# A feed-forward down projection as seven block products, with weight sums on GpSimd

## What is computed

```python
def swiglu(x, w_gate, w_up, w_down):
    return (jax.nn.silu(x @ w_gate) * (x @ w_up)) @ w_down
...
for l in range(DEPTH):
    x = layer_norm(ALPHA * x + FFN_RESIDUAL * swiglu(x, ffn1_w_gate[l], ffn1_w_up[l], ffn1_w_down[l]), ...)
    h = x @ w_in[l]
    ...
    oa = stick_breaking_attention(...)
    ob = chunked_rel_attention(..., rel_bias[l])
    mixed = jnp.concatenate([head_rmsnorm(oa, sb_out_g[l]), head_rmsnorm(ob, ca_out_g[l])], axis=-1)
    x = layer_norm(ALPHA * x + mixed @ w_out[l], ln2_g[l], ln2_b[l])
    x = layer_norm(ALPHA * x + FFN_RESIDUAL * swiglu(x, ffn2_w_gate[l], ffn2_w_up[l], ffn2_w_down[l]), ...)
```

## Time and profile before

| | |
|---|---|
| median of 3 runs | 1040.13 us |
| lowest, highest | 1039.67, 1041.14 us |
| span of the profiled execution (first to last instruction) | 1038.6 us |
| TensorE (PE) busy | 1020.4 us, 98% |
| VectorE (DVE) busy | 585.2 us, 56% |
| ScalarE (ACT) busy | 503.7 us, 49% |
| GpSimd (POOL) busy | 28.3 us, 3% |
| mean granted TensorE clock | 0.998 |

### The profile page before, as it was taken

One profiled execution on the slowest core, in us unless ns is written; L12 is line 12 of the kernel. 1 busy time (PEld: TensorE's weight loads), 2 busy tenths in 40 slices (PEclk: granted clock), 3 DMA queues, 4 the chain that ended last, 5 costly groups with the idle time before them and its releaser, 6 DMA issues.

```text
span 1038.6 us, 18030 instructions
## 1 busy us (share of the span) xinstructions
PE 1020.4 (98%) x7128; PEld 943.2 (91%) x7128; DVE 585.2 (56%) x562; ACT 503.7 (49%) x552; POOL 28.3 (3%) x56
## 2 busy tenths in 40 slices
PE   6999999999999999999989999999999999999999
PEld 6999999799987999999889999997999889999997
DVE  4544544755788554544655454457457975444447
ACT  5444343557685344343543434346576754434335
POOL 3000000001100000000000000000010000000000
PEclk9999999999999999999999999999999999999999
DMA  8755555363325555555455545553623265545451
GB/s 333 282 195 185 179 201 166 119 244 122 123 82 209 202 197 174 189 190 175 161 198 210 185 180 201 172 192 129 232 88 122 87 239 203 187 179 198 171 195 42
DMA packets 34338, 185.24 MB, mean 178 GB/s; under 512 B 3824, under 2 KB 3824, under 8 KB 19440
## 3 DMA queue, kind: packets, MB, share of 16 engines
q1 hardware_dynamic: 32400, 174.60, 47.6%
q0 software_dynamic: 1744, 9.45, 2.5%
q10 hardware_dynamic: 144, 0.52, 0.1%
HBM read 183.51 MB, written 1.05 MB: 178 GB/s over the span
## 4 chain that ended last, share of the span: by engine, by line
PE 98%; DMA 1%; issue 1%; ACT 1%; DVE 0%; SPq 0%; ACTq 0%; DVEq 0%
PE bank L893 29%; PE bank L894 29%; PE bank L895 29%; PE bank L991 8%; PE bank L955 1%; PE bank L938 1%; DMA raw<-stream 1%; PE bank L1107 1%; ACT scratch L407 0%; PE bank L949 0%; DVE xn L715 0%; DVE xT_lo L660 0%; ACT xT_hi L398 0%; ACT w_hi L624 0%; ACT lt L410 0%
## 5 line engine op out<-in xcount | busy, mean ns | idle before, releaser
L640 DVE TENSOR_TENSOR w_lo<-raw,w_hi 128x2048 fp32r<-128x2048 f32 x158 | 361.6, 2292 | 244.8 <-ACT w_hi L380 239.7
L893 PE MATMUL bank<-xT_hi,w_hi 128*128 128x256 f32 x1568 | 444.6, 284 | 0.0
L894 PE MATMUL bank<-xT_lo,w_hi 128*128 128x256 f32 x1568 | 443.7, 283 | 0.0
L895 PE MATMUL bank<-xT_hi,w_lo 128*128 128x256 f32 x1568 | 443.7, 283 | 0.0
L380 ACT ACTIVATE w_hi<-raw 128x2048 fp32r<-128x2048 f32 x158 | 301.2, 1910 | 253.2 <-PE bank L895 241.0
L894 PEld LDWEIGHTS bank<-xT_lo,w_hi 128*128 128x128 f32 x1568 | 300.8, 192 | 1.6
L893 PEld LDWEIGHTS bank<-xT_hi,w_hi 128*128 128x128 f32 x1568 | 300.8, 192 | 1.6
L895 PEld LDWEIGHTS bank<-xT_hi,w_lo 128*128 128x128 f32 x1568 | 300.8, 192 | 0.0
L893 PE MATMUL bank<-w_hi,h_hi 128*128 128x512 f32 x320 | 125.0, 391 | 0.0
L894 PE MATMUL bank<-w_lo,h_hi 128*128 128x512 f32 x320 | 125.0, 391 | 0.0
L895 PE MATMUL bank<-w_hi,h_lo 128*128 128x512 f32 x320 | 124.5, 389 | 0.0
(11 more groups left out here) (127 smaller groups left out, 744.8 us busy)
## 6 DMA issues: line engine op xcount, KB each, us to landing
raw<-stream SPq DMA_DIRECT2D x110, 1024.0 KB, 4.8
raw<-stream SPq DMA_DIRECT2D x110, 512.0 KB, 4.5
lnp<-ln_gb POOLq DMA_DIRECT2D x6, 1024.0 KB, 5.0
soft_t<-rel_band POOLq DMA_DIRECT2D x2, 1024.0 KB, 11.4
xn<-x POOLq DMA_DIRECT2D x1, 1024.0 KB, 7.4
out<-xn SPq DMA_DIRECT2D x4, 256.0 KB, 2.1
qT<-xT SPq DMA_DIRECT2D x1, 512.0 KB, 4.9
qT<-xT ACTq DMA_DIRECT2D x1, 512.0 KB, 5.1
```

What stands on the lines that cost most here:

```text
L640: nc.vector.tensor_tensor(w_lo[:, slot, :], raw[:, slot, :], w_hi[:, slot, :].bitcast(F32), ALU.subtract).then_inc(lo_ready, 1)
L893: nc.tensor.matmul(o, w[0], x[0], start=start, stop=False)
L894: nc.tensor.matmul(o, w[0], x[1], start=False, stop=False)
L895: return nc.tensor.matmul(o, w[1], x[0], start=False, stop=stop)
```

## The change

**Down projection.** For nine of the eleven groups (`SF` = 9) the product of the 256 x 256 block of hidden values (two token blocks times two channel blocks of 128) with the 256 x 1024 block of weights (two channel blocks times two column halves of 512) is formed as Strassen's seven block products, 21 matmuls of 512 columns in place of 24. Each product m accumulates over the nine groups in a PSUM bank of its own (banks 1 to 7); after the nine, VectorE adds and subtracts banks into `xn` and the other two groups are added in the old way on top of four of the banks (`FFN_Y`).

**Sums of operands.** Of the seven weight operands of 512 columns two are plain weights and five are sums or differences, made by GpSimd into `wsum` (which lies in `stick_t`): 1024, 1024 and 512 elements per partition. The seven are split into hi and lo: 3584 elements in place of 2048, in three pieces. Of the seven operands from the hidden values five are sums as well, made by VectorE in four small additions (`h_sums`); 896 elements in place of 512 are split.

**PSUM.** With seven banks taken, gate and up share bank 0: up is computed after SiLU has read the gate, between products 5, 2, 4, 3 and products 1, 6, 7.

**Band.** The host writes `rel_band` flipped and with 8 KB in a row for each partition, straight into `band`; `turn_band` and `band_out` go, `keep_warm(4)` stands in their place. `centred` moves into `qT`.

The diff, cut to its core:

```diff
+SF = FP - 2
+STRASSEN = {1: (5, 6), 2: (2, 1), 3: (6, 3), 4: (0, 2), 5: (1, 0), 6: (4, 5), 7: (3, 4)}
...
+        wsum = flat(stick_t)[:, 0:5 * 512]
+        hs = flat(soft_t)[:, 0:9 * P].rearrange("p (i t) -> p i t", i=9)
...
+            def weight_sums(l, f):
+                base = FFN_BASE[f]
+                with pool.Fori(0, SF) as j:
+                    wait_alone(raw_ready[1], loaded(l, 1, FILLED[base + 4] + j))
+                    wait_alone(lo_ready, split(l, base + 3 * j + 1))
+                    r = raw[:, 1, :].rearrange("p (c d) -> p c d", c=2)
+                    nc.gpsimd.tensor_tensor(wsum[:, 0:1024], r[:, 1, :], r[:, 0, :],
+                                            ALU.subtract).then_inc(wsum_done, 1)
+                    nc.gpsimd.tensor_tensor(wsum[:, 1024:2048].rearrange("p (c d) -> p c d", c=2),
+                                            r[:, :, 0:512], r[:, :, 512:1024], ALU.add).then_inc(wsum_done, 1)
+                    nc.gpsimd.tensor_tensor(wsum[:, 2048:2560], r[:, 1, 0:512], r[:, 0, 512:1024],
+                                            ALU.add).then_inc(wsum_done, 1)
...
                 pool.dma_start(mixg[:, :], mix_g[l]).then_inc(att_par, 16)
-                src = bass.AP(rel_band.tensor, l * (HEADS * BAND), [[1, P], [BAND, HEADS], [1, T]])
-                pool.dma_start(flat(soft_t)[:, 0:HEADS * T].rearrange("p (h s) -> p h s", h=HEADS),
-                               src).then_inc(att_par, 16)
+                pool.dma_start(band[:, :, :], rel_band[l]).then_inc(att_par, 16)
                 wait_alone(att_par, (l + 1) * 32)
                 nc.gpsimd.tensor_scalar(mixg[:, :], mixg[:, :], -0.5, None, ALU.mult).then_inc(gain_ready, 1)
-                wait_alone(band_turned, (l + 1) * 4)
                 nc.gpsimd.memset(band[0:64, :, 192:256], NEG).then_inc(band_ready, 1)
+                weight_sums(l, 0)
                 load_lnp(l, 1)
...
+                def h_sums(j):
+                    dve.wait_ge(hf_done, it(l, f, j) + 1)
+                    nc.vector.tensor_tensor(hs[:, 2:4, :], hs[:, 7:9, :], hs[:, 0:2, :], ALU.add)
+                    nc.vector.tensor_tensor(hs[:, 4, :], hs[:, 0, :], hs[:, 1, :], ALU.subtract)
+                    nc.vector.tensor_tensor(hs[:, 5, :], hs[:, 8, :], hs[:, 7, :], ALU.subtract)
+                    nc.vector.tensor_tensor(hs[:, 6, :], hs[:, 7, :], hs[:, 1, :], ALU.add).then_inc(hsum_done, 1)
...
+                def step(j, start=False, stop=False):
+                    n = strassen(l, f, j)
+                    finished = m_done if stop else None
+                    gate(j, start)
                     pe.wait_ge(hlo_done, it(l, f, j) + 1)
+                    pe.wait_ge(lo_part, 2 * n + 1)
+                    product(5, start, finished)
+                    product(2, start, finished)
+                    pe.wait_ge(lo_part, 2 * n + 2)
+                    product(4, start, finished)
+                    product(3, start, m_done if stop else parts_used)
+                    up(j, bank[0])
                     pe.wait_ge(lo_ready, split(l, base + 3 * j + 4))
-                    down(1, h_hi, h_lo, 0, (0, 1), start=start).then_inc(unit_used, 1)
+                    product(1, start, finished)
+                    product(6, start)
+                    product(7, start, unit_used)
...
+                gate(SF)
+                pe.wait_ge(m_read, (2 * l + f) * 8 + 5)
+                up(SF, bank[4])
```

More of the change, by code:

```diff
@@ L159, in trunk @@
         Y = [[bank[4], bank[5]], [bank[6], bank[7]]]
+        M = {k: bank[k] for k in range(1, 8)}
+        FFN_Y = [[M[7], M[5]], [M[2], M[6]]]
         Z = [bank[2], bank[3]]
-        refine = [sg, hf]
+        refine = [sg, spare]
         SS = [bank[2], bank[3]]
@@ L746, in step, with next_h @@
                     split_lo(l, base + 3 * j + 5, 2)
-                    gated(it(l, f, j) + 1, 3 * j + 3)
-                with dve.Fori(0, FP - 2) as j:
-                    step(j)
-                    split_lo(l, base + 3 * j + 6, 0)
-                step(FP - 2)
-                h_low(it(l, f, FP - 1), hl_hi, hl_lo)
+                def next_h(j):
+                    gated(j + 1, 3 * j + 3, bank[0])
+                    h_sums(j + 1)
+                    split_lo(l, base + 3 * j + 6, 0)
@@ L902, in columns @@
                         w = slice(kc * 256 + c * P, kc * 256 + (c + 1) * P)
-                        last = three(out_bank[:, c * T:(c + 1) * T], (w_hi[:, slot, w], w_lo[:, slot, w]),
+                        last = three(out_bank[:, c * T:(c + 1) * T], (w_hi[:, at(slot, w)], w_lo[:, at(slot, w)]),
                                      (xT_hi[:, kc, :], xT_lo[:, kc, :]), kc == 0, kc == KC - 1)
@@ L927, in down, with pair @@
                             last = three(Y[tb][half][:, :], (hi[:, c0 + c, t], lo[:, c0 + c, t]),
-                                         (w_hi[:, slot, w], w_lo[:, slot, w]),
+                                         (w_hi[:, at(slot, w)], w_lo[:, at(slot, w)]),
                                          start and c == 0, stop and c == 1)
+                return last
+            def pair(slot, h, tb, half, stop=False):
+                for c in range(2):
+                    a = 2 * c + tb
+                    w = at(slot, slice(c * D + half * 512, c * D + half * 512 + 512))
+                    last = three(FFN_Y[tb][half][:, :], (h[0][:, a, :], h[1][:, a, :]), (w_hi[:, w], w_lo[:, w]),
+                                 False, stop and c == 1, True)
                 return last
@@ L1000, in ffn, with gate @@
                 first_columns(l, base, count)
-                columns(l, base + 1, 1, bank[1])
-                def gate_up(j):
+                columns(l, base + 1, 1, bank[7])
+                def gate(j, first=False):
                     pe.wait_ge(silu_done, it(l, f, j) + 1)
+                    if not first:
+                        pe.wait_ge(hf_done, it(l, f, j) + 1)
                     columns(l, base + 3 * j + 2, 2, bank[0])
-                    pe.wait_ge(hf_done, it(l, f, j) + 1)
-                    columns(l, base + 3 * j + 3, 0, bank[1])
@@ L1009, in step, with up @@
-                def step(j, start):
-                    gate_up(j)
-                    pe.wait_ge(hlo_done, it(l, f, j) + 1)
-                    pe.wait_ge(lo_ready, split(l, base + 3 * j + 4))
-                    down(1, h_hi, h_lo, 0, (0, 1), start=start).then_inc(unit_used, 1)
-                step(0, True)
-                with pe.Fori(1, FP - 2) as j:
-                    step(j, False)
-                gate_up(FP - 2)
+                def up(j, into):
+                    pe.wait_ge(silu_done, it(l, f, j) + 2)
+                    columns(l, base + 3 * j + 3, 0, into)
@@ L1020, in ffn @@
+                step(0, start=True)
+                with pe.Fori(1, SF - 1) as j:
+                    step(j)
+                step(SF - 1, stop=True)
+                gate(SF)
+                pe.wait_ge(m_read, (2 * l + f) * 8 + 5)
+                up(SF, bank[4])
                 pe.wait_ge(hlo_done, it(l, f, FP - 1))
                 pe.wait_ge(lo_ready, split(l, base + FFN_UNITS - 2))
+                pe.wait_ge(m_read, (2 * l + f) * 8 + 8)
+                hl = [t[:, :, :].rearrange("p c (b t) -> p (c b) t", b=2) for t in (hl_hi, hl_lo)]
@@ L1022, in ffn @@
                 for tb in range(2):
-                    last = down(1, h_hi, h_lo, 0, (tb,))
+                    for half in range(2):
+                        last = pair(1, (h_hi, h_lo), tb, half)
                     if tb == 1:
@@ L1029, in ffn @@
                     for half in range(2):
[L1030 removed]
+                        pair(2, hl, tb, half, True).then_inc(y_done, 1)
                 last_used(phase(l, 2 * f), 1)
@@ L1187, in _ @@
                 turn_x(0, phase(l, 1))
-                for i in range(3):
-                    turn_band(l, i)
+                keep_warm(4)
                 turn_x(1, phase(l, 1))
-                turn_band(l, 3)
                 attention(l)
```

228 lines of the change are left out of this document (152 added, 76 removed).

## The result

The changed kernel took 1172.3 us (median of 4 runs, 1165.7 to 1176.1) against 1040.6 us of before (1039.7 to 1041.4): 1.126 times the time, 95% interval 1.122 to 1.130. That is slower, as forecast, but 56 us over the forecast of 1116 and 6 us over the upper end of the range. The profiled execution has a span of 1168.3 us; its own time was 1169.9.

The account below looks back on a forecast made before the run. TensorE, busy 1020.4 of 1038.6 us, was the bound. 1038.6 - 26.0 saved + 70.2 waits in three FFNs + 32.0 in layer 0's first = 1114.8 us span, 1116 us with 1.5 to the median; range 1039 to 1166 us.

Parts of the forecast that it names:

- What bounds the kernel; what goes: TensorE bounds; 36 steps lose three matmuls each, 24.6 us, and the band's flip goes: together 26.0 us.
- The flip of the band: Stretch between FFN and next first product shrinks from 7.25 to 6.50 us, twice: 1.4 us.
- GpSimd's sums: Three weight sums per step at 2.2 ns per element: 2.3, 2.3 and 1.2 us, 5.8 us in all.
- The port: VectorE instructions with two SBUF inputs and GpSimd instructions reading SBUF wait for each other; handed over 0.13 us early.
- The loop that results: Slot 1's load, GpSimd's sums and VectorE's work make 18.4 us per step against TensorE's 16.30: 2.1 us waiting.
- Rival 1: Port not held between two arithmetic instructions: loop 16.0 us, no repeated wait, 1042 us; chance 0.14.
- rival 2: Port not held and sums at 0.9 ns per element: faster, near 1034 us; chance 0.11.
- rival 3: Port held, sums at 0.9 ns per element: 1039 us; chance 0.07.
- First steps and ends: TensorE waits 4.4 us at an FFN's first step, 13 in layer 0's first FFN for the band, 0.8 at ends.
- The clock: Waits of 4 to 13 us lower TensorE's granted clock; nothing added, since a slower gate only shortens the wait behind it.
- What would show it: Signs: sums near 2.3, 2.3, 1.2 us, stretched subtractions, slot 1 loads 18.4 us apart, TensorE waits some 2 us on `gated`.
- The range: From 1039 to 1166 us, covering the bounds of the sums' price and Rival 1, leaving out 0.17.

Follow-up runs that it names:

- experiment 8: Kernel before with only the band part: host-laid band loaded straight into its tile, `keep_warm(4)` for the flip; 1040.0 us, ratio 0.9991.
- experiment 2: Changed kernel with GpSimd's three weight sums replaced by fills of nearly the same length that read nothing; 1068.8 us.
- experiment 1: Changed kernel with product 7 of each Strassen step issued four times, nine more matmuls per step; 1169.6 us.
- experiment 6: Changed kernel with weight sums on VectorE, first two pieces split behind `h_sums`, slot 1's load issued early, band wait ahead of nothing; 1047.5 us, 1.0062 times before.
- experiment 7: Kernel of experiment 6 with step 0's up unit ahead of all seven products and no SiLU wait at the last up unit; 1026.3 us, 0.9863 times before.

## Why the prediction was right in direction and short in size

- **What bounds the kernel; what goes.** Right for the products. With nothing in TensorE's way the steps last 16.32 us (forecast 16.30, before 16.98). The flip of the band was priced at 1.4 us; experiment 8's trace shows 0.8.
- **GpSimd's sums.** Right: 2.40 us for 1024 elements alone (2.3 taken), about 1.3 for 512 (1.2). The Trainium skill's figure, halved from 2048 to 1024 elements ("GPSIMD Engine Reference", "Performance versus the Vector engine"), gives an estimate of 2.25 us, near what is measured.
- **The port.** Right, and shown by experiment 2. Rival 1 (not held between two arithmetic instructions) and with it rival 2 are out by the rows above; rival 3 by the sums' length.
- **The loop that results: the step that failed.** Its links and their order were right, its length wasn't: 18.4 forecast, 19.9 measured. The load was sized 4.8 us by the median of loads that stand 5.5 us apart, although the same part frees slot 1 only two links behind slot 0 (`h_lo` and the last piece). It measured 5.34 to its landing (+0.5), and 0.40 more passed until GpSimd started, a term that was put at nothing. The first sum measured 2.68 instead of 2.3 (+0.4), and issue took 0.16. So a step was 3.6 us longer than TensorE's 16.3, not 2.1: some 46 us of the 53.5.
- **First steps and ends.** 4.4 us on `h_lo` forecast, 28.4 - 14.2 = 14.2 for three, 4.7 each; 0.8 at each end, exactly; 13 for the band, 14.2 measured.
- **The clock.** "I add nothing" was right in substance: experiment 1 gives the clock back and gains nothing of note. One detail was missing. A slow gate isn't quite free: it delays VectorE's subtraction into GpSimd's first sum, and through the port the sum took 3.2 us in the step shown and 3.9 at most. Where the others are no bound, as in experiment 6, the clock does cost, some 2 us per FFN by the difference taken there.
- **What would show it.** Nearly all as written, but the signs were matched by TensorE's waits (103.1 against 102.2) although the steps were 1.5 us too long: at half clock TensorE's own work fills the difference. The distance of the loads, also on that list, showed the miss.
- **The range** ended at 1166, from the price of the sums alone. The load, which stood as one value from one median, had no bounds in it. With 4.8 to 5.7 us there, from issue to first sum, its upper end would have been 32 x 0.9 = 29 us higher.

Open: why the load of slot 1, at the same distance behind slot 0's, takes 5.2 us to the first sum in one step and 6.7 in another, and the 8 us outside the steps. Also open is what keeps 11.6 of the 26.0 us from arriving in experiment 7. 6.2 are the two waits shown.

## What to carry to other kernels

Before work goes to an idle engine, draw the loop of its buffers: what frees the input, what it waits for, who comes next, and which of these share a port. GpSimd was idle 97% of the time and still couldn't take 6 us of each step, since they stood in such a loop and shut VectorE out; with the same work on VectorE, 56% busy before, and its order fitted to it, the kernel was 46 us faster. Size a transfer by rows in which its neighbours are as close as the change will put them, and count from its issue to the start of what uses it.
